# The last tile of each stage, its sums of squares and the next norm in two pieces of tokens

## The reference

```
def rms_norm(x, g):
    y = xf * lax.rsqrt(jnp.mean(xf * xf, axis=-1, keepdims=True) + EPS)
    return (y * g.astype(jnp.float32)).astype(x.dtype)
...
        h = rms_norm(x, g_mix[li]) * (1.0 + m_lat[1]) + m_lat[0]
        p = h @ w_in[li]
        ...
        x = x + m_lat[2] * (y @ w_out[li])
        h = rms_norm(x, g_ffn[li]) * (1.0 + m_lat[4]) + m_lat[3]
        x = x + m_lat[5] * conv_ffn(h, ffn_up[li], ffn_conv[li], ffn_conv_b[li], ffn_down[li])
```

## Time and profile before

| | |
|---|---|
| median of three runs | 3944.88 us (3943.88 to 3952.45) |
| the profiled execution's own time | 3946.62 us |
| its span in the trace | 3944.8 us |
| TensorE busy | 3826.0 us, 97% |
| VectorE, ScalarE, GpSimd busy | 1752.3, 1442.9, 1182.1 us |
| mean granted TensorE clock | 0.991 |

### The profile page before, as it was taken

The page is one execution under the profiler, slowest core; times in us unless marked ns, Lnnn a source line. Parts: engine busy times, 40 slices in busy tenths (PEclk is TensorE's granted clock), DMA queues, the critical chain, the costliest instruction groups (busy, mean ns, idle before and its releaser), DMA issues.

```text
span 3944.8 us, 60802 instructions
## 1 busy us (share of the span) xinstructions
PE 3826.0 (97%) x25984; PEld 3056.6 (77%) x25984; DVE 1752.3 (44%) x2693; ACT 1442.9 (37%) x2298; POOL 1182.1 (30%) x697
## 2 busy tenths in 40 slices
PE   8989999999999999999999999999999999999998
PEld 6866778888887678887677788788876777887886
DVE  3366332323354743435856423444368463234333
ACT  3246432322334643332443333433334433334333
POOL 0010221222301033342333236433423322363333
PEclk9999999999999999999999999999999999999999
DMA  5113232322113122222111122222221111222222
GB/s 219 65 51 123 70 123 102 118 71 70 63 65 120 44 88 96 102 75 86 56 42 40 34 84 98 97 88 101 86 81 54 39 40 39 91 104 89 96 92 79
DMA packets 60204, 323.54 MB, mean 82 GB/s; under 512 B 6048, under 2 KB 6176, under 8 KB 34080
## 3 DMA queue, kind: packets, MB, share of 16 engines
q1 hardware_dynamic: 59936, 319.65, 23.3%
HBM read 317.53 MB, written 2.10 MB: 81 GB/s over the span
## 4 chain that ended last, share of the span: by engine, by line
PE 86%; DVE 5%; issue 3%; ACT 2%; DMA 1%; POOL 1%; SPq 0%; DVEq 0%; POOLq 0%; ACTq 0%
PE ps L1604 53%; PE ps L1615 4%; PE ps L760 3%; PE ps L791 3%; PE ps L2666 3%; PE ps L2300 2%; PE ps L1103 2%; PE ps L3168 1%; PE ps L1138 1%; PE ps L2741 1%; PE ps L2763 1%; PE ps L1118 1%; DMA adab<-in_wada 1%; PE ps L2761 1%; PE ps L2288 1%
## 5 line engine op out<-in xcount | busy, mean ns | idle before, releaser
L1576 POOL TENSOR_TENSOR PWL<-ring,PWH 128x1024 fp32r<-128x1024 f32 (+2 forms) x114 | 260.3, 2283 | 640.9 <-ACT PWH L1562 640.8
L1990 DVE SCALAR_TENSOR_TENSOR ftmp<-ps,vec,ftmp 128x511 f32<-128x511 f32 (+2 forms) x440 | 301.7, 695 | 332.1 <-ACT ftmp L1944 213.9
L1576 POOL TENSOR_TENSOR WL<-ring,WH 128x1024 fp32r<-128x1024 f32 (+3 forms) x102 | 227.3, 2229 | 604.8 <-ACT WH L1562 604.8
L1562 ACT ACTIVATE PWH<-ring 128x1024 fp32r<-128x1024 f32 (+2 forms) x216 | 211.9, 983 | 448.3 <-PE ps L1604 404.9
L1562 ACT ACTIVATE WH<-ring 128x1024 fp32r<-128x1024 f32 (+3 forms) x160 | 158.6, 992 | 538.7 <-PE ps L1604 507.6
L1604 PE MATMUL ps<-FH,WH 128*128 128x512 f32 x1008 | 305.7, 358 | 0.0
L1604 PE MATMUL ps<-FH,WL 128*128 128x512 f32 x1008 | 304.4, 356 | 0.0
L1604 PE MATMUL ps<-FL,WH 128*128 128x512 f32 x1008 | 303.7, 355 | 0.0
L1569 DVE TENSOR_TENSOR PWL<-ring,PWH 128x1024 fp32r<-128x1024 f32 (+2 forms) x102 | 125.3, 1230 | 344.2 <-ACT PWH L1562 344.1
L1576 POOL TENSOR_TENSOR PW3L<-ring,PW3H 128x1024 fp32r<-128x1024 f32 (+2 forms) x90 | 204.2, 2269 | 246.3 <-ACT PW3H L1562 246.0
L2013 POOL TENSOR_TENSOR ftmp<-ftmp 128x512 f32<-128x512 f32 (+1 forms) x88 | 126.1, 1433 | 228.2 <-DVE ftmp L1990 227.9
(11 more groups left out here) (623 smaller groups left out, 9937.2 us busy)
## 6 DMA issues: line engine op xcount, KB each, us to landing
ring<-in_wup SPq DMA_DIRECT2D x88, 1024.0 KB, 4.8
ring<-in_wgate SPq DMA_DIRECT2D x24, 1024.0 KB, 4.8
ring<-in_wada SPq DMA_DIRECT2D x22, 1024.0 KB, 4.8
ring<-in_wdown SPq DMA_DIRECT2D x24, 896.0 KB, 4.6
adab<-in_wada SPq DMA_DIRECT2D x40, 512.0 KB, 5.6
ring<-in_win SPq DMA_DIRECT2D x18, 1024.0 KB, 4.8
ring<-in_wout SPq DMA_DIRECT2D x16, 1024.0 KB, 4.8
ring<-in_wdown SPq DMA_DIRECT2D x12, 1024.0 KB, 5.0
```

What stands on the lines that cost most here:

```text
L1562: e.activation(wh, view, ACT.Copy).then_inc(*whi_a.up(L, n))
L1576: e.tensor_tensor(wl, view, wh.bitcast(F32), SUB).then_inc(*wlo_g.up(L, n))
L1990: e.scalar_tensor_tensor(out=dst, in0=src, scalar=conv_cols(L, ch, a), in1=dst, op0=MUL, op1=ADD).then_inc(*(ffn_v.up(L, "tap", x, j, c) i ...
```

## The change

The 512 tokens are handled at the end of each stage as two pieces of 256 (in stage 0 as 512 tokens and 256 context tokens). `segs_of` now gives the pieces and `wide_of` the undivided form.

```diff
+        def tensor_fed_pieces(e, w, L, n, outs, operands, after, order=None):
...
+            for i, out in enumerate(outs):
+                for at, k in enumerate(order):
+                    h, lo = operands(k, i)
+                    for x, (ww, t) in enumerate(((wh, h), (wh, lo), (wl, h))):
+                        mm = e.matmul(out, ww[:, k, :], t, start=at == 0 and x == 0, stop=at == len(order) - 1 and x == 2)
...
+                    after(i, at)
...
+        def tensor_end(e, w, L, tag, total, last, *ready):
+
+            def after(i, at):
+                if (i, at) == (1, 0):
+                    for x in range(2):
+                        tensor_sum_seven(e, w, tag, L, x, total, *ready)
+                if (i, at) == (1, 2):
+                    tensor_sum_last(e, w, tag, L, 0, last)
```

```diff
+        def scalar_two_pieces(high, root, last_square):
+
+            root(0)
+            for k in range(8):
+                high(k, 0)
+                if k == 1:
+                    last_square()
+                if k == 4:
+                    root(1)
...
+            for i in range(2):
+                for k in range(9):
+                    if k < 8:
+                        plain(k, i)
+                    if k:
+                        low(k - 1, i)
+                    if (i, k) == (0, 1):
+                        vector_out_residual(e, w, L, 7, 1)
```

The feed of the third weight view of the next stage moves from behind tile 7 to between the two pieces of the norm. The feeds of the first two views of a mixer stage move ahead of tile 7's residual, into slots that are free by then (`if jj == 6: ... scalar_feed(e, w, L + 1, v)`). `tensor_keep` is gone from all these places. In the FFN of stage 0 the first `next(beside)` moves:

```diff
                     if x == 0:
...
+                        tensor_fed_two_pieces(e, w, L, n, [ffn_psum(L, "up", 0, j) for j in range(2)], operands,
+                                              lambda k, i: [split_a.at(L, "fh", k, i)], lambda k, i: [split_v.at(L, "fl", k, i)], before, after)
                         next(beside, None)
-                        for j in range(2) if L == 0 else (0,):
-                            free("up", 0, j)
-                        tensor_keep(e, w, 2 * (TURN[L]["up", 0, 0] % 3), 5 if L else 2)
-                        tensor_fed_two(e, w, L, n, [ffn_psum(L, "up", 0, j) for j in range(2)], pieces, lambda k: f_high(L, k),
-                                       lambda k: f_low(L, k))
                         next(beside, None)
```

And the output is written by five transfers in place of one:

```diff
-            w.wait_ge(u_v.at((4, "out"), 7, 0))
-            e.dma_start(d["out"], HL[:, :, :]).then_inc(out_sem, 16)
+            parts = [(0, 0, 4), (0, 4, 8), (1, 0, 4), (1, 4, 6), (1, 6, 8)]
+            for i, a, b in parts:
+                c = 256 * i
+                w.wait_ge(u_v.at((4, "out"), b - 1, i))
+                e.dma_start(d["out"][:, a:b, c:c + 256], HL[:, a:b, c:c + 256]).then_inc(out_sem, 16)
```

More of the change, by code:

```diff
@@ L352, in gpsimd_sums, with scalar_last_square @@
                 e.tensor_tensor(total, total, mine, ADD).then_inc(*sq_g.up(tag, "sum", k))
[L354 to L360, removed]
+        def scalar_last_square(e, w, tag, L, i, buf, *ready):
+            x, c, n, _ = segs_of(L)[i]
+            w.wait_ge(*ready)
+            e.activation(buf[:, c:c + n], x[:, 7, :], ACT.Square).then_inc(*sq_a.up(tag, 7, i))
@@ new lines, in tensor_sum_seven, with tensor_sum_last @@
+        def tensor_sum_seven(e, w, tag, L, i, total, *ready):
+            _, c, n, _ = segs_of(L)[i]
+            w.wait_ge(sq_g.at(tag, "sum", 6), *ready)
+            e.matmul(bank(6 + i)[:, 0:n], C("ones"), total[:, c:c + n], start=True, stop=False)
+        def tensor_sum_last(e, w, tag, L, i, buf):
+            _, c, n, _ = segs_of(L)[i]
+            w.wait_ge(sq_a.at(tag, 7, i))
+            e.matmul(bank(6 + i)[:, 0:n], C("ones"), buf[:, c:c + n], start=False, stop=True).then_inc(*sum_mm.up(tag, 7, i))
@@ L619, in scalar_mix_norm @@
             scalar_proj_feed(e, w, l, 2)
[L620 to L624, removed]
+            scalar_lam(e, w, l)
         def h_split(l, k, context):
@@ L704, in scalar_proj_feed @@
                 elif l:
[L705 removed]
+                    w.wait_ge(fed.at(0, len(VIEWS[0]) - 1) if v == 2 else mod_mm.at(*MOD_PARTS[-1], "part"))
                 elif v == 2:
@@ L1759, in vector_ffn_norm, with plain @@
-            for k in range(9):
-                if k < 8:
-                    plain(k)
-                if k:
-                    low(k - 1)
+            def plain(k, i):
+                X, c, m, s = segs_of(L)[i]
+                w.wait_ge(norm_a.at("inv", (L, "ffn"), i))
+                if L == 0 and k >= 4:
+                    w.wait_ge(split_v.at(0, "fl", k - 4, i))
+                e.scalar_tensor_tensor(out=f_plain(L, k)[:, c:c + m], in0=X[:, k, :], scalar=GF[:, k, s:s + 1] if L < 2 else
+                                       vc("norm_ffn_2", 8 * (L - 2) + k), in1=f_root(L, i), op0=MUL,
+                                       op1=MUL).then_inc(*u_v.up((L, "ffn"), k, i))
@@ new lines, in low @@
+            def low(k, i):
+                c = 256 * i
+                w.wait_ge(h_a.at((L, "mix"), k, i))
+                e.tensor_tensor(h2_low(k)[1][:, c:c + 256], h2_low(k)[0][:, c:c + 256], PXH[:, k, c:c + 256].bitcast(F32),
+                                SUB).then_inc(*hs_v.up((L, "mix"), k, i))
+            for i in range(2):
+                for k in range(9):
+                    if k < 8:
+                        plain(k, i)
+                    if k:
+                        low(k - 1, i)
+                    if (i, k) == (0, 1):
+                        vector_ffn_residual(e, w, L - 1, 7, 1)
```

359 lines of the change are left out of this document (241 added, 118 removed).

## The result

The changed kernel took 3958.27 us (median of 7 runs), the kernel before 3948.59 (7 runs beside it). The ratio of their runs is 1.0036, with a 95% interval of 1.0025 to 1.0047: slower by 0.36%, some 14 us. A second measurement gave 1.0051 (1.0034 to 1.0067), some 20 us. I had said 3947 us, with 3938 to 3955 as the range.

The account below looks back on a forecast made before the run. TensorE, 86% of the chain, was taken to bound the kernel. The terms summed to a 1.9 us loss on the profiled 3946.6, giving 3948.5; that run was 1.7 above the median, so 3947 us, range 3938 to 3955.

Parts of the forecast that it names:

- stage 0, to the tile behind the parts: Stage 0's w_out end through modulation parts 0 and 1: 3.5 us lost, plus 1.7 for the clock.
- `w_out`, stages 1, 2, 3: Ends of w_out with the norm in two pieces: 0.7 us lost in stage 1, 0 in stages 2 and 3.
- clock of the three sums: TensorE's 1.9 us waits at the first sum in stages 1 to 3: half of 1.7 us each, 2.6 lost.
- mixer norms: Norms at the ends of ffn_down, ahead of the next mixer: 0.7 us gained into stage 1, 0.5 twice after.
- the end: Program's end: 1.5 us gained by earlier scaling and 3.4 by a last transfer of 256 KB, together 4.9.
- GpSimd beside the norm: Third weight's low part on GpSimd beside piece 1 slows VectorE's low parts: 0.5 us lost in stages 2 and 3 each.
- The clock: Idle TensorE drops to 1.2 GHz for 3.4 us, losing 1.7: once in stage 0, half for each of three sums.
- Parts 0 and 1: Stage 0's first modulation parts, now behind the paired tiles: TensorE idles about 6 us for part 1's weights, 3.5 lost.
- The sum and the root: Early sum at the w_out end, stage 2: TensorE waits 1.9 us, VectorE starts scaling 1.7 us sooner.
- Full durations on VectorE: Rival: VectorE's full instruction durations add up in the paired tiles, 2.6 us at five ends, 3960 us; chance 0.05.
- The clock rival: Rival: every TensorE wait at three sums, two mixers and stage 0 drops the clock, 7.7 us more, 3955; chance 0.14.

Follow-up runs that it names:

- e7: Changed kernel with part 0 between the pieces, splits and sums reordered, and stage 0's modulation-part transfers issued ahead of the weight load: 0.9960 of the kernel before.
- e2_third_on_vector: Changed kernel with the low part of each FFN's third weight made by VectorE behind the norm instead of by GpSimd: 1.0032 of the kernel before.
- e3: Changed kernel with tile 6's residual, square and total ahead of the weight splits at the end of w_out: 1.0032 of the kernel before.
- e8: Kernel before with only stage 0's modulation-part transfers issued ahead of the weight load in SyncE's queue: 0.9983 of the kernel before.

## Why the prediction was wrong

The sum had a loss, and there was one, but of 14 to 20 us and not of 1.9. Term by term, in us, gains positive, measured by the marks in the two pairs of traces:

| term | forecast | measured |
|---|---|---|
| stage 0, to the tile behind the parts, its clock included | -5.2 | -7.9, -9.7 |
| stage 0, the FFN's later parts | none | -5.5, -4.1 |
| `w_out`, stages 1, 2, 3 | -0.7, 0, 0 | -5.8, -2.0, -3.4 and -3.1, -2.0, -3.4 |
| clock of the three sums | -2.6 | in the row above |
| mixer norms, stages 1, 2, 3 | +1.7 together | +2.8, +1.4 together |
| the end | +4.9 | +4.8 |

The kernel before has this row of GpSimd beside the 2.05 us of the earlier trace rows:

```profile
1813.47 1.29 POOL L2192 TENSOR_TENSOR ar<-ar,XC 128x512 f32<-128x512 f32 x1 [4.74 <-PE ps L2137]
```

- **The failed step: GpSimd beside the norm.** I wrote that three or four low parts "slowed so cost 0.5 us, in stages 2 and 3 each", with 0.9 as the upper bound. It cost a TensorE gap of 1.84 to 1.94 us in each of stages 1 to 3, and 2.2 of VectorE's time in stage 0. I had read the 2.05 us of the earlier trace rows as a slower instruction. It is a hold. GpSimd's instruction beside it was over at 1814.76, and VectorE's split, started at 1813.79, ended 1.08 behind that at 1815.84, nearly its own 1.23. Had I compared ends and not durations, the bound would have been GpSimd's whole 2.4 us. The Trainium skill says it outright in another place than the one I used (SBUF — State Buffer, SBUF: two separate sides): the shared port pair is a lock that is held for the whole instruction, and the loser waits. By the trace (2.40 us with the split in one piece, 1.33 and 1.50 in halves) it holds here.
- **A term left out: the later parts.** I followed SyncE's queue to part 1 and put the parts behind it at nothing, without a reason. The same queue cost 4 to 5 us there, removed by e7.
- **The clock, under-sized and in the wrong place.** I charged 1.7 for stage 0 and half of 1.7 for each of three sums. Stage 0 had 10.2 us at 1.2 GHz and not 3.4, and in the FFN behind it there were 6.8 and 3.4 us. Of the six waits at sums in the two traces (three ends of `w_out` each) one was followed by 3.4 us of low clock, at 1435.4 in stage 1. Of the six gaps behind the hold, which I had not priced at all, three were: at 1452.5 in stage 1, and in stage 3 in both traces, where it costs 1.4 (68.7 without, 70.2 with it). With the hold removed, in e2_third_on_vector, neither stage had any.
- **Parts 0 and 1, right in mechanism.** From the pair's end to the next tile I had 9.5 us; it is 10.4 (497.12 to 507.52). The landing was 4.9 us and not 5.6, which low clock and the pause ahead of L470 made up for. But the pair ended at 499.6 on the time axis of the kernel before and not at 497.5: these 2.1 us are the hold again.
- **The sum and the root, right.** The wait at L376 is 1.7 to 2.1 where I said 1.9. In stage 2 scaling starts 8.3 us behind the start of tile 7 (2502.35 to 2510.68), forecast 2492.2 - 2484.0 = 8.2. A block and piece takes 0.73 to 0.74, forecast 0.74. The tiles end 24.8 behind that start, forecast 22.4: the hold's 1.9 and 0.5 more.
- **Mixers and end, right,** with a slip. 0.6 and 0.8 against 0.5, but the terms I wrote down add up to 1804.2 for the copy and not 1804.6, which would be 0.9. Into stage 1 it is 0.1 to 1.4 against 0.7; the end 4.8 against 4.9, of which the transfers are 3.4 as said. (The first paragraph's "96 products" is a slip too: the row has x48, and its 11.0 us are 48 x 0.230.)
- **The rivals.** Full durations on VectorE did not occur. The clock rival had the right sign and much of the size, but it put the low clock behind the sums and the mixers' waits; most of it lay at the parts and behind the hold.

## What to carry over

When work moves beside other work, look for which instructions of the two engines may not run together, and price the meeting by the longer instruction, since the one that starts second waits for its end. When a norm or a tile is cut in pieces, everything queued between (weight splits, totals, side work) has to be ordered anew for the earlier piece: here the change lost 14 to 20 us with the old order and, with a new one and five transfers, gained 9 to 11. And where whole runs scatter by some us, the distance between the same two instructions in two traces tells tenths.

## What the runs showed of the hardware

A VectorE instruction (`TENSOR_TENSOR`, `SCALAR_TENSOR_TENSOR`) that reads two tensors from SBUF and starts while GpSimd works gets no further until GpSimd's instruction is over: 2.40 us instead of 0.42, 2.31 instead of 0.48. It then takes nearly its own length: it ends 0.28 us behind GpSimd for 256 columns, 0.55 for 512, 1.08 for 1024. The trace of the kernel before had it already: of the VectorE instructions that started inside a GpSimd instruction with more left than their own length, all 17 of this kind were held, and all 10 `CAST` and `TENSOR_SCALAR` with one input from SBUF. None was that had an input in PSUM (323 cases; 0.42 beside a running 2.38 us split, in e3), and none of the 82 `TENSOR_REDUCE`, `MAX8`, `MATCH_REPLACE8` and `RECIPROCAL` from SBUF. It goes both ways: GpSimd's total of 768 columns took 2.89 us instead of 1.85 ahead of stage 1, where it started together with a VectorE split of 1.22. And two transfers of 512 KB, issued directly behind a weight load in the same queue, took 5.5 to 8.3 us to land, and 3.5 to 5.8 when nothing stood ahead of them (6.7 once, in e8).
